# Pieces of w_ada in the place of x: two more slots, a second load of x, and all late pieces in pairs within IN

## The reference, cut to what matters

```python
c_act = jax.nn.silu(c)                       # [1, 2048]
mod = c_act @ w_ada[l] + b_ada[l]            # w_ada: [2048, 12288]
sh1, sc1, gt1, sh2, sc2, gt2 = jnp.split(mod, N_MOD, axis=-1)
h = modulate(rmsnorm(x, g_norm_mix[l]), sh1, sc1)
proj = h @ w_in[l]                           # IN
...                                          # convolution, recurrence, pools
y = jnp.concatenate([y_lru, y_pool], axis=-1) @ w_out[l]   # OUT
x = x + gt1[:, None, :] * y
h = modulate(rmsnorm(x, g_norm_ffn[l]), sh2, sc2)
...                                          # feed-forward, then the second block
```

## Time and profile before

| | us |
|---|---|
| median of 3 runs | 2589.31 |
| lowest, highest | 2587.9, 2591.44 |
| the profiled execution | 2592.49 |
| its span in the trace | 2590.3 |
| TensorE busy (share of the span) | 2525.4 (97%) |
| VectorE busy | 1781.5 (69%) |
| ScalarE busy | 1180.1 (46%) |

### The profile page before, as it was taken

The page is one execution under the profiler, slowest core; times in us unless marked ns, Lnnn a source line. Parts: engine busy times, 40 slices in busy tenths (PEclk is TensorE's granted clock), DMA queues, the critical chain, the costliest instruction groups (busy, mean ns, idle before and its releaser), DMA issues.

```text
span 2590.3 us, 39847 instructions
## 1 busy us (share of the span) xinstructions
PE 2525.4 (97%) x14556; PEld 2149.9 (83%) x14556; DVE 1781.5 (69%) x2300; ACT 1180.1 (46%) x1439; POOL 17.5 (1%) x52
## 2 busy tenths in 40 slices
PE   5999999999999999999999999999999999999998
PEld 1677688888888888888888888888888888888887
DVE  3368698955555555688686665676788668876886
ACT  2345435444444444564444554445544444444444
POOL 0000000000000000000000000000000000000000
PEclk7999999999999999999999999999999999999999
DMA  9978987955555555566555455556555655555554
GB/s 389 396 277 339 384 322 272 340 176 190 190 187 186 189 190 188 163 192 205 185 174 171 163 171 193 186 184 192 181 180 183 204 184 194 185 189 181 191 165 127
DMA packets 156809, 554.48 MB, mean 214 GB/s; under 512 B 16400, under 2 KB 20496, under 8 KB 156704
## 3 DMA queue, kind: packets, MB, share of 16 engines
q1 hardware_dynamic: 155376, 549.85, 61.9%
q0 software_dynamic: 1328, 3.21, 0.5%
HBM read 550.37 MB, written 2.10 MB: 213 GB/s over the span
## 4 chain that ended last, share of the span: by engine, by line
PE 87%; DVE 5%; DMA 5%; ACT 2%; issue 1%; SPq 0%; DVEq 0%; ACTq 0%
PE ps L562 53%; PE ps L569 26%; DMA ride<-in_w_ada 5%; PE ps L559 2%; PE pm L590 1%; DVE split L1240 1%; PE ps L566 1%; ACT split L899 1%; DVE acc_out L1293 0%; PE pm L610 0%; DVE x_t L1396 0%; DVE val L1253 0%; DVE h_s L1600 0%; PE pm L598 0%; DVE h_s L1374 0%
## 5 line engine op out<-in xcount | busy, mean ns | idle before, releaser
L1240 DVE TENSOR_TENSOR split<-raw,split 128x1024 fp32r<-128x1024 f32 (+1 forms) x864 | 1031.0, 1203 | 698.3 <-ACT split L899 695.2
L899 ACT ACTIVATE split<-raw 128x1024 fp32r<-128x1024 f32 (+1 forms) x864 | 896.5, 1043 | 1154.0 <-PE ps L569 1082.7
L562 PE MATMUL ps<-h_s,split 128*128 128x512 f32 x3880 | 1232.2, 399 | 6.5 <-DVE h_s L1374 3.8
L569 PEld LDWEIGHTS ps<-h_s,split 128*128 128x128 f32 x3880 | 732.8, 189 | 173.8
L569 PE MATMUL ps<-h_s,split 128*128 128x256 f32 x3880 | 765.6, 279 | 0.0
L562 PE MATMUL ps<-mid_s,split 128*128 128x512 f32 x2336 | 736.1, 396 | 0.5 <-DVE split L1240 0.4
L562 PEld LDWEIGHTS ps<-h_s,split 128*128 128x128 f32 x3880 | 595.7, 190 | 24.0 <-issue 18.4
L569 PEld LDWEIGHTS ps<-mid_s,split 128*128 128x128 f32 x2336 | 439.5, 188 | 104.1
L569 PE MATMUL ps<-mid_s,split 128*128 128x256 f32 x2336 | 459.6, 278 | 0.0
L562 PEld LDWEIGHTS ps<-mid_s,split 128*128 128x128 f32 x2336 | 356.3, 189 | 4.6 <-issue 2.6
L906 ACT ACTIVATE low<-ps 128x512 f32<-128x512 f32 x230 | 133.4, 580 | 0.0
(11 more groups left out here) (266 smaller groups left out, 1197.8 us busy)
## 6 DMA issues: line engine op xcount, KB each, us to landing
raw<-in_w_in SPq DMA_DIRECT2D x224, 512.0 KB, 3.5
ride<-in_w_ada SPq DMA_DIRECT2D x64, 1024.0 KB, 9.1
raw<-in_w_ffn_down SPq DMA_DIRECT2D x128, 512.0 KB, 4.1
raw<-in_w_ffn_gate SPq DMA_DIRECT2D x88, 512.0 KB, 3.3
raw<-in_w_ffn_up SPq DMA_DIRECT2D x88, 512.0 KB, 4.1
raw<-in_w_ffn_a SPq DMA_DIRECT2D x88, 512.0 KB, 4.1
raw<-in_w_ffn_b SPq DMA_DIRECT2D x88, 512.0 KB, 4.4
raw<-in_w_out SPq DMA_DIRECT2D x64, 512.0 KB, 5.4
```

What stands on the lines that cost most here:

```text
L562: pe.matmul(ps[:, s, b, :], split[:, slot, k, 0, b * P:(b + 1) * P], acts[:, k0 + k, :, :].rearrange("p h t -> p (h t)"), start=start, sto ...
L569: mm = pe.matmul(ps[:, s, b, 0:T], split[:, slot, k, 1, b * P:(b + 1) * P], acts[:, k0 + k, 0, :], start=False, stop=stop)
L899: act.activation(split[:, c, 0:kt, 0, :], raw[:, CHUNKS * s + c, 0:kt, :], ACT.Copy).then_inc(hi_ready, 1)
L1240: dve.tensor_tensor(split[:, c, 0:kt, 1, :], raw[:, CHUNKS * s + c, 0:kt, :], split[:, c, 0:kt, 0, :].bitcast(F32), ALU.subtract).then_inc ...
```

## The change

The late pieces get four slots instead of two (`LATE_SLOTS`): slots 4 and 5 are the two halves of `x_t`, slots 0 and 1 the old ones. A pair takes 4 and 5, the next 0 and 1, and so on. The first pair in `x_t` waits for the norm's last block (`norm_t`). The late pairs ride behind every second chunk, 17, 19, 21 and so on to 47, all within IN. Since x is overwritten, SP loads it a second time when the last pair in `x_t` (pair 45) has been multiplied, and VectorE waits for that load before the residuals of OUT. The computation is the same.

```diff
--- before.py
+++ after.py
@@ -68,7 +68,7 @@
 PIECES = DB // 2
 EARLY = 2
 EARLY_RING = 4
-LATE_RING = 2
+LATE_SLOTS = (4, 5, 0, 1)
 
 
 HALF_SLABS = 8
@@ -87,11 +87,12 @@
 def _rides():
 
     at = [1, 1, 3, 3, 5, 5, 6, 6, 8, 8, 10, 10, 12, 12, 13, 13]
-    at += [HALF_CHUNKS + (r | 1) + r // 4 for r in range((TENSOR_PARTS - 4) * PIECES)]
+    at += [HALF_CHUNKS + (r | 1) for r in range((TENSOR_PARTS - 4) * PIECES)]
     return at
 
 
 RIDE_AT = _rides()
+X_AGAIN = RIDE_AT[-3] + RAW
 LAST_RIDE = {n: RIDE_AT[PIECES * (n - EARLY) + PIECES - 1] for n in range(EARLY, TENSOR_PARTS)}
 ADD_AT = [50 + 26 * j // 32 for j in range(OUT_ADDS)] + [CHUNKS * 22 + j for j in range(2 * DB)]
 LAST_ADD = {n: ADD_AT[DB * (n - TENSOR_PARTS) + DB - 1] for n in range(TENSOR_PARTS, ADA_PARTS)}
@@ -200,8 +201,8 @@
 
 
     WPAD = 16
-    ride = at("ride", [P, LATE_RING, 2, ADA_COLS], F)
-    ride_2 = at("ride_2", [P, EARLY_RING - LATE_RING, 2, ADA_COLS], MID + 16384)
+    ride = at("ride", [P, 2, 2, ADA_COLS], F)
+    ride_2 = at("ride_2", [P, 2, 2, ADA_COLS], MID + 16384)
     pool_x = at("pool_x", [P, 4, 2, WPAD + T], F + 16384)
     row = at("row", [P, 512], F + 25088)
     add_out = at("add_out", [P, OUT_ADD_RING, ADA_COLS], H_AT)
@@ -247,17 +248,22 @@
     pm = [ctx.enter_context(nc.psum_tensor(f"pm{k}", [P, 512], F32)) for k in range(4)]
 
     def ada_slot(slot):
-        return ride[:, slot, :, :] if slot < LATE_RING else ride_2[:, slot - LATE_RING, :, :]
+
+
+        if slot >= 4:
+            return x_t[:, 8 * (slot - 4):8 * (slot - 3), :].rearrange("p (e b) t -> p e (b t)", e=2)
+        return ride[:, slot, :, :] if slot < 2 else ride_2[:, slot - 2, :, :]
 
     def ada_place(piece):
+
 
         first_late = 4 * PIECES
         if piece < first_late:
             return piece % EARLY_RING, piece // EARLY_RING + 1, piece - EARLY_RING + 1
-        slot, turn = (piece - first_late) % LATE_RING, (piece - first_late) // LATE_RING
-        before = first_late // EARLY_RING
-        last = piece - LATE_RING if turn else first_late - EARLY_RING + slot
-        return slot, before + turn + 1, last + 1
+        slot, turn = LATE_SLOTS[(piece - first_late) % 4], (piece - first_late) // 4
+        if slot >= 4:
+            return slot, turn + 1, piece - 3 if turn else 0
+        return slot, first_late // EARLY_RING + turn + 1, piece - 3 if turn else first_late - EARLY_RING + slot + 1
 
     def add_slot(j):
 
@@ -290,7 +296,7 @@
     tables_loaded = sem("tables_loaded")
     ident_loaded = sem("ident_loaded")
     constants = sem("constants")
-    ada_loaded = [sem(f"ada_loaded{k}") for k in range(EARLY_RING)]
+    ada_loaded = [sem(f"ada_loaded{k}") for k in range(6)]
     c_ready = sem("c_ready")
     rows_ready = sem("rows_ready")
     add_loaded = [sem(f"add_loaded{k}") for k in range(OUT_ADD_RING)]
@@ -431,8 +437,14 @@
                 if at + min(RAW, 3 + at // 2) == G:
                     piece = EARLY * PIECES + r
                     slot, _, free = ada_place(piece)
-                    sp.wait_ge(ada_multiplied, free)
+                    if free > 0:
+                        sp.wait_ge(ada_multiplied, free)
+                    else:
+                        sp.wait_ge(norm_t, DB)
                     load_ada(slot, piece // PIECES, piece % PIECES)
+            if G == X_AGAIN:
+                sp.wait_ge(ada_multiplied, TENSOR_PARTS * PIECES - 2)
+                sp.dma_start(x_t[:, :, :], dram["x_fm"].rearrange("(b p) t -> p b t", p=P)).then_inc(x_loaded, 16)
             for j, at in enumerate(ADD_AT):
                 if at == G - RAW:
                     where, slot, _ = add_slot(j)
@@ -1660,6 +1672,7 @@
                 finish_rides(CHUNKS * (S_OUT + q) + c)
             return mid
         dve.wait_ge(mod_ready, 6)
+        dve.wait_ge(x_loaded, 32)
         for q in range(OUT_SLABS):
             residual_turn(S_OUT + q, q, 2, 1, (S_OUT + q) // 2, q % 2, mid=out_mid(q))
         dve.wait_ge(ident_loaded, 16)
```

## The result

| | median, us | lowest to highest | runs |
|---|---|---|---|
| before, beside it | 2590.01 | 2587.04 to 2594.17 | 22 |
| after | 2594.57 | 2592.69 to 2597.96 | 22 |

The ratio is 1.0017 with a 95% interval of 1.0011 to 1.0024: slower by 4.6 us, a hair within the 0.2% that the prediction called "no change". Forecast were 2591.6, which is 2.3 above the median of 2589.3 that was known then, and a range of 2580 to 2600. The profiled execution of the changed kernel took 2594.16 us with a span of 2592.0; before it was 2592.5 and 2590.3.

A forecast was written before the change was run, and what follows sets the result against it. TensorE, busy 97% of the span, was taken as the bound, with VectorE setting OUT's end. 2592.5 - 4.6 (IN) - 11.2 + 5.7 (pairs moved) + 9.7 (pair 47) + 2.7 (clock) = 2594.8, less 3.2: 2591.6 us; range 2580 to 2600.

The forecast's parts named there:

- Pair 47 held up: End of IN: pair 47's load queues behind x's; 9.7 us idle, landing at p + 15.8, p being pair 45's start on TensorE.
- The rival in which the pair isn't held up: End of IN: pair 47 comes in time, so the 9.7 and 2.7 go: 2579.2 us; chance 0.13.
- The offset: Whole kernel: 3.2 us taken off the sum because before's profiled execution lay that far above its runs' median, 2589.3.
- The low end of this term: Pair 47's wait at the end of IN: smallest idle time, given as 9.3 us from 2.0 + 3.1 + 5.1 + 5.1 - 7.6 + 1.5.
- Half clock behind it: Behind pair 47's wait: TensorE's clock falls, costing 1.8 us in chunk 48 plus the second piece's slowdown, 2.7 in all.
- IN: Chunks 16 to 47: 4.6 us of TensorE waits go, three moved pairs add 5.7 us.
- The rival of an IN bound by the DMA: IN, pairs 17 to 47: at 340 GB/s the loads set the time, +8, giving 2600 us; chance 0.05.
- OUT: First matmul of OUT to second column sum: VectorE sets the end, 102.9 us falls to 91.7, a loss of 11.2.
- the term of -4.6: IN: all TensorE waits go, 2.7 us for w_ada loads, 1.4 for ScalarE's gate, 0.5 for VectorE's pool block.
- "same": Whole kernel: the measured time lies within about 0.2% (5.2 us) of before, bounds 2584.1 and 2594.5; chance 0.53.
- The rival of an OUT that doesn't shorten: OUT: VectorE's slabs cost 13.9 us instead of 12.83, five times 1.1 are gone: 2597.1 us; chance 0.17.

The follow-up runs named there:

- e1: The changed kernel with the second load of x issued right behind pair 47's load, nothing else changed: 2585.1 us, ratio 0.9982 to before.
- e7: The kernel before with both column sums of OUT one chunk later, nothing else: 2587.5 us, ratio 0.9985 to before.
- e8: The kernel before, unchanged, profiled once more: 2595.2 us in one run.
- e10: e1 with 30 of OUT's 32 VectorE additions on 512 of 1024 columns: 2576.6 us, ratio 0.9949 to before.
- e5: The kernel before with two slots, no second x load, late pairs at every second chunk from 17 to 47: 2588.9 us, ratio 0.9995 to before.
- e9: e5 with both column sums of OUT one chunk later: 2585.5 us, ratio 0.9975 to before.
- e6: e1 with both column sums of OUT, and VectorE's use of them, one chunk later: 2582.0 us, ratio 0.9962 to before.
- e4: The changed kernel, reloading only the first of x's 16 blocks at the same place: 2589.1 us, ratio 0.9995 to before.

## Why the prediction was right or wrong

**Pair 47 held up: right.** Forecast 9.7 us of idle time, measured 8.09 + 0.67 = 8.8. The first piece was multiplied at p + 15.78, forecast 15.8. The second stands 2.56 us behind it, as in the row that I took it from; only, the first ran at half speed too, so that less of the 2.56 was idle. OUT began at p + 20.15, where the prediction's terms give 15.8 + 2.56 + 1.89 = 20.2. x landed in 8.7 us. The Trainium skill, DMA: Bandwidth & Descriptors, section Queues, rings and completion order, has descriptors taken in ring order; a landing within 0.1 us of the sum in order of issue agrees with it, and the early finish that it allows for didn't show. The rival in which the pair isn't held up, at 2579.2, is what e1 made true by one line, at 2585.1. The offset of 3.2 and OUT's 3.5, less 0.6 in IN, all three below, make 6.1, near the 5.9 between. (The low end of this term adds up to 9.2 in the prediction's own figures, not 9.3.)

**Half clock behind it: right in kind.** Forecast 2.7, one piece and three steps of chunk 48. Measured: two pieces, 3.77 less 2.08 = 1.7, and three steps that take 3.82 (283.07 to 286.89) for 2.14, another 1.7: 3.4.

**IN: right.** No wait from 140 to 262 us. The forecast for IN+ without pair 47 was -4.6 + 5.7 = +1.1 against before; e1 measured +0.5. Against e7 and e8, in whose executions the loads gave less idle time, it is +2.4 and +2.0, so the 4.6 of waiting is itself a figure with a scatter of 2 us. The rival of an IN bound by the DMA is out: in e1 the window of IN has 371 GB/s with TensorE never idle (window of e1).

```profile
140.00:262.00 122.00, 122.00 (x756) 88.03 (x752) 90.20 (x134) 59.45 (x91) 0.00 (x0) 1.00 0.97 371
```

The Trainium skill, DMA: Bandwidth & Descriptors, section Where 436 GB/s comes from, has some 358 GB/s as the bound of loads from HBM, as one core's half of a stack; this trace, with one core running, doesn't agree, with 371 over 122 us.

**OUT: the mechanism was right up to the second sum, the term was mis-sized.** Forecast 91.7, and with the 1.8 of half clock that fall into it 93.5; measured 93.9 in after. That looks good and isn't: in e1, which has no pause, it is 95.2 against 91.7. VectorE's evacuations tell where. The timeline of VectorE in after (line 1265 is the evacuation of before's line 1253):

```profile
301.01 0.68 DVE L1265 TENSOR_TENSOR val<-ps,low 128x512 f32<-128x512 f32 x1
...
313.58 0.69 DVE L1265 TENSOR_TENSOR val<-ps,low 128x512 f32<-128x512 f32 x1
...
365.38 0.68 DVE L1265 TENSOR_TENSOR val<-ps,low 128x512 f32<-128x512 f32 x1
...
376.82 0.69 DVE L1265 TENSOR_TENSOR val<-ps,low 128x512 f32<-128x512 f32 x1
```

The five slabs from 301.01 to 365.38 are 64.37, forecast 64.2. The last four chunks are 11.6 (365.38 to 376.96), forecast 9.9. That is a slip in my own rows: I counted slabs from evacuation to evacuation and the last one from the split behind it, and dropped the 1.5 us between (363.71 to 365.23). The start, from the first matmul to the first evacuation, was forecast at 10.6 + 7.0 = 17.6, or 19.4 with the half clock. In e1 it is 19.3 (271.38 to 290.66), 1.7 too long; in after it is 17.9, 1.5 shorter than forecast, since VectorE and ScalarE had caught up. In e1 VectorE gets its split at 285.06, 13.7 behind the first matmul where I had 10.6, after 4.13 us of idle time; the split had waited for TensorE, and TensorE 1.12 us for a row that ScalarE copies at the end of IN, which no term of mine held. Behind that short wait the clock fell (window of e1), and chunk 50's four steps took 4.4 us (279.28 to 283.71) in place of 2.85, another 1.6. That leaves 0.4 of the 3.1 us; 1.4 of them are made good up to the evacuation.

```profile
280.00:282.00 2.00, 2.00 (x9) 0.50 1.03 410
```

(This view is of TensorE alone: its busy time, then clock, DMA and GB/s.)

From the first evacuation to the second sum e1 has 75.95 and after 75.95: with the sums at this place the chain is a fixed length, and only its start moves. So e1 misses by 1.7 + 0.2 + 1.7 = 3.6, and in after the start hides 1.5 of what the rest misses. The gain of OUT, forecast 11.2, was 7.65 in e1.

The whole sum, against before's execution: IN with the moved pairs +0.5 (forecast +1.1), pair 47 +8.8 (9.7), its pieces at half clock +1.7 (0.9), OUT with its half clock -9.0 (-11.2 + 1.8). That is +2.0 from terms and +2.2 by the stretches of the table; the execution as a whole took 2594.16, +1.7, where the sum said 2594.8.

**The offset: the step that failed.** I then took 3.2 us off, since before's profiled execution lay that far above its median, and came to 2591.6 where the median is 2594.6. The other profiled executions don't lie above theirs: after's is 0.4 below, those of e1 to e10 are between 1.5 below and 1.0 above, apart from before's own second one, which is 3.9 above. Without the offset the forecast would have been off by 0.2 us, in part by luck, since terms were off by up to 1.7 us either way. Before's first profiled execution was not outside the spread of its runs (2587.0 to 2594.2), and part of its excess can be placed: its IN+ was 131.95, against 130.44 and 130.05 in e8 and e7, which issue the same up to OUT. These 1.5 to 1.9 us are waits for loads, and the term of -4.6 had taken all such waits off already, so that this part was subtracted twice. The second one's 3.9 is another matter: 2.7 of it is clock behind the second sum, and e5 had that too without lying above its median. What is left of either, and whether before's executions lean or only scatter, stays open.

The chances: "same" had 0.53, and the measured ratio is at its upper edge. The rival of an OUT that doesn't shorten fell (slabs of 12.87 on average, not 13.9), though its price of 5.5 us was partly paid in other coin, the late start and the last slab.

What each part is worth by itself, from pairs of runs: the pairs moved -1.6 to -2.0 (before beside e5, and e7 to e9, whose baselines differ by 0.6; the first lies within its uncertainty), two more slots -3.8 and -3.5 (e5 to e1, e9 to e6, by medians; the timelines show the second and only 1.0 of the first), x's load at its place +9.5 (e1 to after; 9.1 by their ratios). The change is a gain of 5.4 us with one load in the wrong turn.

## What to carry to other kernels

A load that must wait belongs behind every load on its queue that is needed sooner; ask of each wait that is put on an in-order queue what stands behind it, for here one line of that kind was worth 9.5 us, more than all the rest of the change. Slots beyond the landing time buy independence from late landings rather than speed, so judge them by the worst landing and not by the median one. And don't correct a sum by the distance of one profiled execution from the median: a second profile of before lay even higher and would have confirmed the wrong correction. Find in the trace where the excess lies, and ask whether a term of the sum has taken it off already.

## What the runs showed of the hardware that I had not expected

- The same instructions on the same data had median landings of 6.2 us in one execution and 7.1 in another (e5, e9), and before had 6.9 and 6.6. With two slots that moved 4.5 us of TensorE's time.
- Short waits can cost as much again in clock: behind 2.29 + 1.53 us of waiting with one piece between them the granted clock was 0.50 for 4 us (e4). But before's five waits of 6.2 us in all in front of pairs 49 to 54 left it at 1.00. What tells the two apart wasn't tried. In e1 a single wait of 1.12 us was followed by 0.50 from 280 to 282 us, and cost 1.6 more.
- Behind nearly the same wait the lower clock lasts unequally long: after a wait of 1.30 us (e1) TensorE's matmuls behind the second column sum were at half speed until about 371.9, 5.3 us after the sum's start; after 1.28 us (e5) until about 377.0, 8.0 us after it.
- The pause of after isn't all lost: VectorE and ScalarE go on, and with 12.2 us lost on TensorE ahead of chunk 48 and in it (8.8 and 3.4), the stretch to the second sum came out 9.4 longer than e1's.
